# One tile's gates by accumulating scatter DMAs, and a shorter one-hot stage

## The reference

```
q = (x @ w_q).reshape(tokens, 8, 256)
s1, s2 = q[..., :128] @ sub_k1.T, q[..., 128:] @ sub_k2.T
t1, i1 = top_k(s1, 16);  t2, i2 = top_k(s2, 16)
top_s, pos = top_k(t1[..., :, None] + t2[..., None, :], 16)   # over 256 pairs
ids  = (i1 * 128 + i2) at pos                                 # 16 experts a head
gate = softmax(top_s)
hid  = gelu(x . u[ids])
out += sum over heads and picks of gate * hid * v[ids]
```

## Time and profile before

| | us |
|---|---|
| median of three runs | 1973.86 |
| profiled execution, its time | 1973.14 |
| its span | 1971.3 |
| retrieval, 686 to 1223, in the span | 537 |
| gate stage with its tail, 1223 to 1436 | 213 |
| experts, 1436 to the end | 535 |

### The profile page before, as it was taken

How to read it: one execution, slowest core, us unless ns; L and a number is a source line. 1 busy time by engine, 2 the same in 40 slices (tenths; PEclk the granted TensorE clock), 3 DMA queues, 4 the chain that set the end, 5 groups by cost and what they waited for, 6 DMA issues and landing times. The chain is left out here.

```text
span 1971.3 us, 35045 instructions
## 1 busy us (share of the span) xinstructions
PE 1896.8 (96%) x13809; PEld 1657.6 (84%) x13809; DVE 1477.1 (75%) x3142; ACT 756.0 (38%) x1165; POOL 362.0 (18%) x337
## 2 busy tenths in 40 slices
PE   8999999899999899999999998999789999999999
PEld 8999887677854689999999998998668888888887
DVE  5353335766662369999999999999878888888887
ACT  5322445222240234433443343776433333333332
POOL 2001100011100003213331330000433222322221
PEclk9999999999999999999999999999999999999999
DMA  4222101100040348668867974287789999999996
GB/s 160 86 87 74 44 22 65 56 3 3 3 172 32 132 132 328 241 235 331 312 236 256 345 278 144 87 268 217 253 336 361 338 337 338 349 337 338 338 339 249
DMA packets 176116, 407.25 MB, mean 207 GB/s; under 512 B 16848, under 2 KB 100048, under 8 KB 175312
## 3 DMA queue, kind: packets, MB, share of 16 engines
q1 hardware_dynamic: 133040, 255.96, 37.9%
q0 software_dynamic: 39744, 144.72, 19.4%
q10 hardware_dynamic: 3168, 4.33, 0.6%
HBM read 358.77 MB, written 46.14 MB: 205 GB/s over the span
## 5 line engine op out<-in xcount | busy, mean ns | idle before, releaser
L89 PE MATMUL eo_ps<-vh,e_wh 128*128 128x512 f32 x768 | 300.3, 391 | 8.7 <-DVE e_wl L2062 8.7
L90 PE MATMUL eo_ps<-vh,e_wl 128*128 128x512 f32 x768 | 299.7, 390 | 0.0
L91 PE MATMUL eo_ps<-vl,e_wh 128*128 128x512 f32 x768 | 299.7, 390 | 0.0
L2028 POOL DMA_INDIRECT e_rows<-in_v,gidx x128 | 140.3, 1096 | 386.3 <-DVE e_acc_t L2042 352.7
L1651 POOL DMA_INDIRECT g_stage<-in_u_rows,gidx x112 | 135.5, 1210 | 391.4 <-DVE gidx L1746 236.8
L2011 ACT CAST vh<-vraw 128x1024 fp32r<-128x1024 f32 x96 | 100.7, 1049 | 235.2 <-PE eo_ps L91 230.2
L89 PE MATMUL h_ps<-x2h,h_uh 128*128 128x384 f32 x520 | 181.2, 348 | 8.4 <-DVE h_ul L1507 5.3
L89 PEld LDWEIGHTS eo_ps<-vh,e_wh 128*128 128x128 f32 x768 | 144.8, 189 | 40.2 <-DVE vl L2053 5.6
L1503 ACT ACTIVATE h_hid<-h_ps 128x384 f32<-128x384 f32 x128 | 63.5, 496 | 290.6 <-PE h_ps L91 209.5
L91 PE MATMUL h_ps<-x2l,h_uh 128*128 128x384 f32 x520 | 174.9, 336 | 0.0
L89 PE MATMUL h_ps<-x2h,q_uh 128*128 128x384 f32 x504 | 170.6, 339 | 4.5 <-ACT h_hid L1503 4.5
(11 more groups left out here) (318 smaller groups left out, 4304.0 us busy)
## 6 DMA issues: line engine op xcount, KB each, us to landing
vraw<-in_v SPq DMA_DIRECT2D x96, 512.0 KB, 6.2
g_stage<-in_u SPq DMA_DIRECT2D x63, 512.0 KB, 6.6
h_uraw<-in_u SPq DMA_DIRECT2D x45, 512.0 KB, 5.4
wraw<-in_w_z SPq DMA_DIRECT2D x43, 512.0 KB, 3.5
HID_scratch<-h_hid SPq DMA_DIRECT2D x106, 192.0 KB, 4.0
e_hid<-HID_scratch SPq DMA_DIRECT2D x96, 192.0 KB, 6.6
G_scratch<-g_stage SPq DMA_DIRECT2D x16, 1024.0 KB, 12.0
g_hot<-in_v SPq DMA_DIRECT2D x32, 512.0 KB, 6.3
```

The source lines that it names most:

```text
L89: nc.tensor.matmul(out, a[0], b[0], start=start, stop=False)
L90: nc.tensor.matmul(out, a[1], b[0], start=False, stop=False)
L91: return nc.tensor.matmul(out, a[0], b[1], start=False, stop=stop)
L2028: nc.gpsimd.indirect_dma_start(rows[:, j % GBUF_E], None, d["v"].rearrange("c p n -> (c p) n"), bass.IndirectOffsetOnAxis(ap=gidx[:, j:j + ...
```

## The change

Tile 0's part of G is no longer made by one-hots. Its place in DRAM is cleared early, by SP in the recurrence, with eight DMAs from a tile of zeros:

```
+            sp.wait_ge(zeroed, 1)
+            for r in range(GPARTS):
+                a = slice(r * NK // GPARTS, (r + 1) * NK // GPARTS)
+                sp.dma_start(keep["G"][a, :, 0:P].rearrange("a b t -> b a t"),
+                             zeros[:].unsqueeze(1).broadcast_to([P, NK // GPARTS, P])).then_inc(keep["g_cleared"], 16)
```

Its gates are then added to it by indirect DMAs from Pool, one for each of the 128 picks, 128 numbers of 4 B in each. The order in the retrieval (after the eight gathers, scatters and gathers alternate):

```
+    def scatter(pool, j, place, weights):
+        if j > 0:
+            pool.wait_ge(keep["g_added"], j * 16)
+        nc.gpsimd.indirect_dma_start(
+            places, bass.IndirectOffsetOnAxis(ap=place, axis=0), weights, None,
+            compute_op=ALU.add).then_inc(keep["g_added"], 16)
...
+            pool.wait_ge(keep["g_cleared"], GPARTS * 16)
+            for h in range(PH - 1):
+                pool.wait_ge(row_listed, h + 1)
+                for k in range(GBUF_R):
+                    gather(h * TOPK + k)
+                pool.wait_ge(listed, h + 1)
+                for k in range(TOPK):
+                    keep["scatter"](pool, h * TOPK + k, places[:, h, k:k + 1], picks[:, 2, 0, h, k:k + 1])
+                    if k + GBUF_R < TOPK:
+                        gather(h * TOPK + k + GBUF_R)
```

VectorE works out the places, with two more operations a head:

```
+                link(nc.vector.scalar_tensor_tensor(out=expert[:], in0=picks[:, 0, :, h], scalar=float(NK),
+                                                    in1=picks[:, 1, :, h], op0=ALU.mult, op1=ALU.add))
+                link(nc.vector.scalar_tensor_tensor(out=places[:, h] if h < PH - 1 else place[:], in0=expert[:, 0], scalar=float(2 * P),
+                                                    in1=token[:].broadcast_to([P, TOPK]), op0=ALU.mult, op1=ALU.add))
+                nc.vector.tensor_copy(gidx[:, picked], expert[:, ND]).then_inc(row_listed, 1)
```

The gate stage has 64 steps, for tile 2 (kept in SBUF) and then tile 1. In each, VectorE makes three of the four weighted one-hots and ScalarE the fourth, as relu(weight - weight x |iota - index|):

```
+            def last_token(n):
+                t = slice(n * TB + TB - 1, n * TB + TB)
+                nc.scalar.activation(away[:], iota[:], ACT.Abs, bias=picksT[:, 0, t], scale=-1.0).then_inc(distance, 1)
+                act.wait_ge(distance, n + 2)
+                nc.scalar.activation(hot1[:, n % 2, TB - 1], away[:], ACT.Relu, bias=picksT[:, 2, t],
+                                     scale=minus[:, n:n + 1]).then_inc(last_made, 1)
```

The chunks beside the steps follow a table: 8 k-slices before the first step, then 3, 3, 2 and again through the first half (86), 2, 1, 1, 1 through the second (40), and 42 behind the steps. The last head's gathers start with the stage, and their dots stand between the steps:

```
+    FILL = ((3, 3, 2), (2, 1, 1, 1))
+    dot_step = [4 + j * 7 // 4 for j in range(TOPK)]
```

Its 16 scatters go between the loads of `u` on Pool, two after each of eight loads. Tile 1's stage is stored in eight parts behind the last step; SP waits for the first part and for all scatters and loads `G[0]` before it leaves the stage:

```
+            sp.wait_ge(staged, STEPS)
+            for r in range(GPARTS):
+                a = slice(r * QA, (r + 1) * QA)
+                sp.dma_start(G[a, :, P:2 * P].rearrange("a b t -> b a t"), second[:, a]).then_inc(keep["g_part"][r], 16)
+                if r == 0:
+                    sp.dma_start(first["v"], d["v"][0]).then_inc(keep["e_v_in"][0], 16)
+                    sp.wait_ge(keep["hid_stored"][0], 16)
+                    sp.dma_start(first["hid"], keep["HID"][0]).then_inc(keep["e_g_in"][0], 16)
+            sp.wait_ge(keep["g_added"], PH * TOPK * 16)
+            sp.wait_ge(keep["g_part"][0], 16)
             sp.dma_start(first["g"], G[0]).then_inc(keep["e_g_in"][0], 16)
```

More of the change, by code:

```diff
@@ L84 @@
 ROWS_FROM = 2
+GPARTS = 8
+ONEHOT = (2, 1)
 def matmul3(nc, out, a, b, start, stop):
@@ L1254, in _ @@
                 sp.dma_start(keep["H2"][:, i], acc[:, i]).then_inc(keep["h2_stored"], 16)
+        @block.gpsimd
+        def _(pool):
+            for n in keep["spent"]:
+                pool.sem_clear(range(n, n + 1))
         @block.tensor
@@ L1617, in _ @@
             act.wait_ge(keep["h2_stored"], 16 * NQ)
+            for m in range(AHEAD):
+                split_hi(act, m + 2)
+                gelu(act, m)
             for b in range(2):
@@ L1862, in _, with gather @@
+            sp.wait_ge(keep["g_part"][0], 16)
             sp.dma_start(first["g"], G[0]).then_inc(keep["e_g_in"][0], 16)
[L1863 to L1864 removed]
         @block.gpsimd
         def _(pool):
[L1868 to L1871 removed]
+            def gather(j):
@@ L1872, in _ @@
                 nc.gpsimd.indirect_dma_start(
                     rows[:, j], None, d["u_rows"],
-                    bass.IndirectOffsetOnAxis(ap=gidx[:, LATE + j:LATE + j + 1], axis=0)).then_inc(rows_in[j // 4], 16)
-            for m in range(TAIL + GSLOT + 1, NCHUNK):
-                load(pool, m)
+                    bass.IndirectOffsetOnAxis(ap=gidx[:, LATE + j:LATE + j + 1], axis=0)).then_inc(rows_in[j], 16)
+            gathers, scatters = iter(range(TOPK)), iter(range(TOPK))
+            for j in itertools.islice(gathers, 2):
+                gather(j)
@@ L1878, in _ @@
+            for m in range(NRC + GSLOT, NCHUNK):
+                load(pool, m)
+                for j in itertools.islice(gathers, 3):
+                    gather(j)
+                if m >= NRC + GSLOT + 5:
+                    for k in itertools.islice(scatters, 2):
+                        keep["scatter"](pool, LATE + k, keep["place"][:, k:k + 1], keep["last_gate"][:, k:k + 1])
+            pool.wait_ge(keep["g_added"], PH * TOPK * 16)
         @block.vector
         def _(dve):
+            split_lo(dve, NRC)
@@ L1921, in _ @@
+            nc.scalar.mul(minus[:], picksT[:, 2, bass.ds(TB - 1, STEPS, step=TB)], -1.0).then_inc(distance, 1)
+            act.wait_ge(distance, 1)
+            for n in range(2):
+                if n > 0:
+                    act.wait_ge(last_made, n)
+                last_token(n)
+            split_hi(act, NRC + 1)
             for n in range(STEPS):
                 tile, i = n // NS, n % NS
-                if n % 4 == 0 and n // 4 <= BESIDE:
-                    split_hi(act, NRC + n // 4)
@@ L1925, in _ @@
-                if tile == 2 and i == 0:
-                    act.wait_ge(g_stored[0], 8 * 16)
+                if n in begins[0:REST - 1]:
+                    split_hi(act, NRC + begins.index(n) + 1)
+                if tile == 1 and i == 0:
+                    act.wait_ge(dotted, TOPK)
                 act.wait_ge(placed, n + 1)
-                nc.scalar.copy(stage[tile % 2][:, :, i * TB:i * TB + TB].rearrange("p a t -> p t a"),
+                nc.scalar.copy(stage[tile][:, :, i * TB:i * TB + TB].rearrange("p a t -> p t a"),
@@ L1940, in experts @@
+                if n in ends or n == 0:
+                    gelu(act, NRC + (ends.index(n) if n > 0 else 0))
+                    store(act, NRC + (ends.index(n) if n > 0 else 0))
+            for i in range(REST):
+                if begins[i] == STEPS and i + 1 < REST:
+                    split_hi(act, NRC + i + 1)
+                if ends[i] == STEPS:
+                    gelu(act, NRC + i)
+                    store(act, NRC + i)
 def experts(nc, d, keep):
@@ L2024, in _ @@
             pool.wait_ge(v_hi, 2)
+            for r in range(GPARTS):
+                pool.wait_ge(keep["g_part"][r], 16)
             for j in range(NPICK):
```

167 lines of the change are left out of this document (92 added, 75 removed).

## The result

| | before | after |
|---|---|---|
| time, median (us) | 1974.01 (4 runs) | 2127.62 (4 runs, 2122.46 to 2134.09) |
| ratio after/before, 95% interval | | 1.0777 [1.0745, 1.0809] |
| span of the profiled execution | 1971.3 | 2125.8 |

The prediction, 1940, was wrong, and the range too. The kernel became 154 us slower.

The account below looks back on a forecast made before the run. TensorE was taken to bound the retrieval and VectorE the gate stage. Terms -35-4.5-1+8 = -32.5 us on a span of 1971.3, plus 1.84, gave 1940.6, predicted as 1940; range 1918 to 2005.

Parts of the forecast that it names:

- Pool's chain: Retrieval: each scatter waits for the one before to land; a head takes Pool 24+15L, 69 us, losing 8 us.
- rival A: Retrieval: Pool's chain just about fits, L up to 3.2 (29 us lost, 1962); forecast 1940, chance 0.50.
- B: Retrieval: Pool's chain becomes the bound, deciding from L = 3.3; at 4.0 113 us lost; 2003, chance 0.30.
- L: Time of each scatter in the retrieval's chain on Pool, taken as 3.0 us, between 2.3 and 4.5.
- The gate stage: VectorE sets the first half (78 us), ScalarE the second (60); last copy 42 us earlier, stage gives 35.
- ScalarE's pair: Gate stage: two chained activations, 0.31+0.03+0.31 us, beside a copy of 0.88, a step of 1.53; no table loads.
- rival C: Gate stage: ScalarE becomes the bound, a step of 1.9 instead of 1.53 us, 14 us more, 1954; chance 0.12.
- The store's tail: After the gate stage's last copy: first expert product at last copy + 35 + 5, a loss of 7 us.
- The front: Retrieval's start: two chunks split and Gelu'd early, 4.5 us gained; fewer transposes and moved copies, 1 us gained.
- The clearing of G: Recurrence: clearing G (8 MB, on SP) costs nothing; 35 us once if its cover fails.
- Rival D: Retrieval and experts: L under 2.8, experts start as soon as 33 us behind the last copy; 1925, chance 0.08.
- The added operations: Retrieval: three VectorE operations where one stood, some 0.5 us a head, under 2.85 us left, so no cost.

Follow-up runs that it names:

- Runs 1 and 2: The changed kernel without its scatters (1): 2013.46 us; with scatters in turn to four places, each waiting for the fourth before it (2): 2015.41 us.
- run 6: The changed kernel with its scatters as plain writes, without addition, in the same chain: 2075.36 us.
- Run 3: The changed kernel with VectorE's split of the next chunk one step later in the gate stage: 2083.18 us.
- run 12: Run 9 with the split three steps behind the chunk's begin instead of one: 1952.68 us.
- run 9: Run 7 with the third chunk's cast and split at step 2, fewer k-slices beside the first half of the steps and three scatters a load: 1965.76 us.
- run 13: Run 12 with all four weighted one-hots on VectorE: 1958.94 us.
- run 10: The kernel before with only the early splits and Gelus of the front (AHEAD = 2): 1966.83 us.
- run 7: The changed kernel, computation whole, scatters waiting only at the first pick of a head, and the split one step later: 1968.04 us.
- run 4: The changed kernel without scatters and with the split one step later: 1968.68 us.

## Why the prediction was wrong

**Pool's chain: the step that failed first.** "I take 3.0", and the choice of rival A over B. The mechanism of B is what happened, as it stands there: rows of u late, VectorE at a dot with the splits behind it, TensorE behind those. Runs 1 and 2 show it. The seven heads took 593.4 us (743.25 to 1336.6), 118 more than before, and B's line for L = 4.0 had 113. That this is so near is luck, two errors against each other: with the measured L the form would have given 171. The form 24 + 15L was too dear: measured it is 17.3 + 14L + 1.9 in the head shown (18.7 in place of 17.3 in the mean), which at my L of 3.0 fits in 61 us and decides at 3.4. And L was 4.55 in the mean of the heads, not 3.0, which is the term that was mis-sized. Three parts of it, of which I had priced one and guessed 0.4 for the others:
- the issue on Pool, 1.55 us for a DMA that adds; I had 0.93, and no row showed one;
- the landing, 1.6 to 1.7 us behind that issue in the quiet, 3.2 to 3.3 in all. This lies between the bounds (2.3 and 4.5), but the mean of 4.55 is above the upper one;
- the traffic: scatters 1 to 8 stand behind a 512 KB gather each, 4.9 us apart (851.20 to 885.28 in seven steps). I wrote this down as an argument for B and then priced L by the quiet row. But scatters 9 to 15, with no gather issued between them, are still 4.2 apart, so the place in Pool's queue is the smaller part of it.

The rule of the Trainium skill (DMA: Bandwidth & Descriptors, "Anatomy of one DMA — SWDGE (gpsimd) path") of about 2.0 us for such a DMA falls short here as well: the closest two plain scatters stand 2.4 us apart in run 6, and the closest two with addition 3.1. I was right not to follow it, and stayed too near to it.

**The gate stage: a term left out.** I counted instructions engine by engine (76, 71 and 70 us in the first half) and took the largest. With three engines within a tenth of each other, the largest is the bound only where the waits between them have slack. "Counting the begins of the chunks" I placed the splits, and did not ask what each waits for: the cast of the same step. That is 216 us instead of 139. Run 3 gave back 48 of the 77, run 12 came to 144.3. Run 12 has the thinner table of run 9, though, for which the same count gives 4.5 us less, 134.7, four splits having left the first half. So the wait was the main error, and the count itself was still 10 us short: 7 in the first half and 3 in the second. A part of the 7 is the start. The eight k-slices ahead of the first step stand in no sum of the prediction, and the first copy began 8.6 us behind the first compare in run 12 and 9.6 in the changed kernel, where it was 3.9 before. I had asked for the wait on Pool's queue, and not on VectorE's.

**ScalarE's pair** takes 0.83 us (1353.09 to 1353.52 to 1353.92), not 0.65, and a step 1.7, not 1.53; rival C had put 1.9. By run 13 the pair cost time only through the splits that waited. No table load stands between Abs, Relu, copy and Gelu, as taken.

**The store's tail** was right: 41.0 us, 40 predicted. The front was 5.75 us (first burst at 743.25 instead of 749.0) where 4.5 and 1 were predicted; run 10 gives 6.8 for it alone. The clearing of G in the recurrence shows no cost in this trace: the first product of the hidden layer starts at 666.5, before it was 666.8. But over the thirteen traces with the clearing this start lies at 669.4 in the mean (666.3 to 673.4), and at 666.8 and 664.2 in the two without, so a few microseconds are not excluded. Rival D did not occur.

**The added operations**, put at nothing: in the runs without the chain's cost a head takes 67.7 us, with scatters (run 7) or without (run 4), and 67.15 before and in run 10, 4 us over the seven heads. TensorE is busy throughout in both, with about the same 378 matmuls, so it is not VectorE's slack that ran out; the cause is open.

**What stays open:** which traffic holds a scatter at 4.2 us when no gather stands before it in Pool's queue; what the 0.55 us more of a head are; and what, beside the start, the 10 us are that the gate stage of run 12 has over the count.

## What to carry to other kernels

A chain of DMAs in which each waits for the last is priced by issue + landing *under the traffic that stands before it in its queue*, and before pricing it one asks whether the data need the chain: here only one link in sixteen was needed, and taking the other fifteen away gave back the whole cost. Where work moves between engines that are nearly full, check for every instruction how many steps lie between it and what it waits for on the other engine; a distance of zero made 216 us of a stage priced at 139, and one step of distance alone brought it to 168. Help from an idle engine may be worth its work only after such waits are gone: the same one-hot cost 10.6 us of the stage before, and gave some 2 behind.

## What the runs showed of the hardware

- An indirect DMA that adds to DRAM holds Pool 1.55 us at the least and 1.59 in the median, one that only writes 0.97 and 1.00, a gather 0.93 and 1.00. All three are DMAs of 128 rows; run 6 and the changed kernel differ by that one argument.
- From issue to landing 2.9 us at least with addition, 2.1 without; the median is 3.9 and 3.6 beside other traffic.
- TensorE stood still from 823.5 to 840.81. In eight microseconds of that the granted clock was 0.54 of full speed, nearly the lower of its two levels (1.2 GHz), where it had been 1.00:

```profile
825.00:833.00 8.00, 0.00 (x0) 0.00 (x0) 0.00 (x0) 0.90 (x1) 4.06 (x3) 0.54 0.17 20
```

From 840.81 to 846.0 it was 0.50, and the 16 matmuls there start 0.32 us apart; behind them they start 0.17 apart again. A stop so costs TensorE some 2.5 us more than its length (5.28 us for 16 starts instead of 2.8, an estimate from these rows). In the retrieval that is hidden, since Pool set the head. Over the gate stage the clock was 0.83 to 0.84; what that cost in time no run here separates.
